# Page loop of a hybrid decoder step: head values, sample products, probability splits and value lower halves are issued in another order

## The reference

```python
def mla_keys(ckv, w_uk, kn_nope):
    return rms_norm(jnp.einsum('...c,chd->...hd', ckv, w_uk), kn_nope)
...
def mla_prompt_attention(q_nope, q_pe, k_nope, k_pe, v):      # 16 heads, 256 tokens, causal
        s = mla_scores(qn, qp, k_nope, k_pe)
        s = jnp.where(k_pos[None, :] <= q_pos[:, None], s, -jnp.inf)
        p = jax.nn.softmax(s, axis=-1)
        return jnp.einsum('bhqk,bkhv->bqhv', p.astype(v.dtype), v)
...
    def page_step(carry, p_idx):                              # 8 requests x 16 cached pages
        phys = page_table[:, p_idx]
        ckv = pool_ckv[phys]
        s = mla_scores(q_nope, q_pe, mla_keys(ckv, w_uk, kn_nope), pool_kpe[phys])
        return merge(carry, s, ckv), None
...
    s = mla_scores(q_nope, q_pe, k_nope_new, k_pe_new)        # the sample's own new position
```

## Time and profile before

| | us |
|---|---|
| time before, median of 3 runs (2768.45 to 2770.84) | 2768.56 |
| the profiled execution, its own time | 2765.64 |
| its span in the trace | 2764.0 |
| PE busy | 2633.9 (95% of the span) |
| DVE busy | 1910.3 (69%) |
| ACT busy | 1341.6 (49%) |

### The profile page before, as it was taken

The page is one execution under the profiler, slowest core; times in us unless marked ns, Lnnn a source line. Parts: engine busy times, 40 slices in busy tenths (PEclk is TensorE's granted clock), DMA queues, the critical chain, the costliest instruction groups (busy, mean ns, idle before and its releaser), DMA issues.

```text
span 2764.0 us, 60668 instructions
## 1 busy us (share of the span) xinstructions
PE 2633.9 (95%) x22232; PEld 2480.3 (90%) x22232; DVE 1910.3 (69%) x3729; ACT 1341.6 (49%) x2759; POOL 227.0 (8%) x327
## 2 busy tenths in 40 slices
PE   7987799999999999999899999979999999999997
PEld 5777689999999999996789999968999999999997
DVE  4656659979996555553667777754997999755554
ACT  2333214457775444443345555541455777544443
POOL 0034100000000000000013333320000000000000
PEclk9999999999999999999899999989999999999999
DMA  5311034544444555554012222213454444455553
GB/s 172 122 54 34 15 122 157 179 166 155 156 158 168 182 182 179 179 213 165 19 36 85 81 81 85 82 47 122 153 178 166 158 156 159 170 179 180 181 182 130
DMA packets 109764, 372.42 MB, mean 135 GB/s; under 512 B 16665, under 2 KB 21018, under 8 KB 109026
## 3 DMA queue, kind: packets, MB, share of 16 engines
q1 hardware_dynamic: 94706, 324.34, 34.0%
q0 software_dynamic: 14832, 45.10, 5.3%
HBM read 365.36 MB, written 4.01 MB: 134 GB/s over the span
## 4 chain that ended last, share of the span: by engine, by line
PE 86%; DVE 8%; ACT 3%; issue 2%; DMA 0%; DVEq 0%; ACTq 0%; POOL 0%; SPq 0%; POOLq 0%
PE ps L795 84%; ACT arena L2273 2%; DVE arena L1496 2%; DVE arena L2092 1%; DVE ring_lo L1496 1%; PE ps L1094 1%; PE ps L1089 1%; DVE arena L1625 0%; DVE arena L1500 0%; DVE arena L2123 0%; DVE v_lo L1496 0%; PE ps L854 0%; ACT L2273 0%; DVE arena L1511 0%; DMA cst<-in_consts 0%
## 5 line engine op out<-in xcount | busy, mean ns | idle before, releaser
L1496 DVE TENSOR_TENSOR ring_lo<-ring,w_hi 128x1024 fp32r<-128x1024 f32 x512 | 624.8, 1223 | 397.7 <-ACT w_hi L2273 394.2
L2273 ACT ACTIVATE arena<-ps 128x256 f32<-128x256 f32 (+18 forms) x981 | 399.1, 426 | 777.6 <-PE ps L795 702.5
L2273 ACT ACTIVATE w_hi<-ring 128x1024 fp32r<-128x1024 f32 x512 | 542.3, 1059 | 385.8 <-PE ps L795 384.7
L795 PE MATMUL ps<-x_hi,w_hi 128*128 128x264 f32 x2048 | 592.8, 289 | 2.8 <-DVE ring_lo L1496 2.8
L795 PE MATMUL ps<-x_hi,ring_lo 128*128 128x264 f32 x2048 | 582.2, 284 | 0.0
L795 PE MATMUL ps<-x_lo,w_hi 128*128 128x264 f32 x2048 | 582.1, 284 | 0.0
L795 PE MATMUL ps<-h_lo,w_hi 128*128 128x264 f32 x2048 | 582.0, 284 | 0.0
L795 PE MATMUL ps<-h_hi,ring_lo 128*128 128x264 f32 x2048 | 581.7, 284 | 0.0
L795 PE MATMUL ps<-h_hi,w_hi 128*128 128x264 f32 x2048 | 579.8, 283 | 1.0 <-issue 1.0
L1496 DVE TENSOR_TENSOR arena<-arena 128x512 f16<-128x512 f16 (+19 forms) x738 | 402.1, 564 | 17.6 <-DVE arena L1496 3.3
L795 PEld LDWEIGHTS ps<-x_hi,w_hi 128*128 128x128 f32 x2048 | 386.6, 189 | 4.3 <-issue 4.2
(11 more groups left out here) (170 smaller groups left out, 2760.9 us busy)
## 6 DMA issues: line engine op xcount, KB each, us to landing
ring<-in_wstream SPq DMA_DIRECT2D x608, 512.0 KB, 3.3
arena<-in_cache_t POOLq DMA_DIRECT2D x128, 128.0 KB, 2.3
arena<-in_cache_n POOLq DMA_DIRECT2D x128, 128.0 KB, 2.3
arena<-in_mla_w POOLq DMA_DIRECT2D x1, 3072.0 KB, 10.2
arena<-in_state POOLq DMA_DIRECT2D x4, 512.0 KB, 4.3
out_wkv_s<-arena POOLq DMA_DIRECT2D x4, 512.0 KB, 4.7
arena<-in_cache_t SPq DMA_DIRECT2D x128, 16.0 KB, 1.7
arena<-in_consts SPq DMA_DIRECT2D x1, 1472.0 KB
```

Source lines behind the costliest of these rows:

```text
L795: return nc.tensor.matmul(out, lhsT, rhs, start=start, stop=stop, **kw)
L1496: return v.tensor_tensor(out, a, b, op)
L2273: return nc.scalar.activation(out, in_, func, **kw)
```

## The change

Four edits, all in the page loop:

1. `products` on PE: six matmuls in the place of 32, two of 64 columns (all heads of one parity in one matmul) and four of 32 columns, into the same bank with the same result. It now stands behind the first third of page 17.
2. `head_values`: on PE head n - 2 behind the first third of page n, in the place of head n - 1 at the end of page n. On DVE head n - 2 ahead of `head_scores(n)`, in the place of head n - 1 behind it.
3. `lower_value` on DVE: right behind `page_sums`, in the place of the end of the loop pass.
4. `prob_sums` is cut in two: `split_probs` at the end of the pass of p = 8, the sum of the probabilities stays at p = 9.

```diff
--- before.py
+++ after.py
@@ -1318,10 +1318,13 @@
 
                 w.next(heads_ready)
                 take(6)
-                for h in range(HEADS):
-                    o = ps[:, 6, h * NS:(h + 1) * NS]
-                    mm(o, C(f"half{h % 2}"), prodn[:, h // 2, :], True, False)
-                    last = mm(o, C(f"quar{h % 4}"), prodr[:, h // 4, :], False, True)
+                acc = dict(skip_group_check=True)
+                by_half = ps[:, 6, 0:P].rearrange("p (c f b) -> p f c b", f=2, b=NS)
+                by_quarter = ps[:, 6, 0:P].rearrange("p (g m b) -> p m g b", m=4, b=NS)
+                for f in range(2):
+                    mm(by_half[:, f], C(f"half{f}"), prodn, f == 0, False, **acc)
+                for m in range(4):
+                    last = mm(by_quarter[:, m], C(f"quar{m}"), prodr, False, m == 3, **acc)
                 last.then_inc(for_dve, 1)
 
             def head_scores(h):
@@ -1413,8 +1416,6 @@
             for b in (1, 2, 4, 5):
                 pe.wait_ge(bank_free[b], taken[b])
             for n in range(PAGES):
-                if n == HEADS + 1:
-                    products()
                 req, p = n // NPAGE, n % NPAGE
                 q = req - 1
                 if p == 0 and req >= 2:
@@ -1423,6 +1424,10 @@
                 pe.wait_ge(pg_ready, n + 1)
                 take(3 * (n % 2), 2)
                 third_keys(n, 0)
+                if 2 <= n < HEADS + 2:
+                    head_values(n - 2)
+                if n == HEADS + 1:
+                    products()
                 if q >= 0:
                     if p == 4:
                         turn_max(q)
@@ -1444,8 +1449,6 @@
                     head_turns(n - 1)
                 if n < HEADS:
                     head_scores(n)
-                if 1 <= n <= HEADS:
-                    head_values(n - 1)
             for j in range(2):
                 for half in range(2):
                     b = 2 * j + half
@@ -2148,13 +2151,16 @@
                 own(tt(sm(3, q), sm(3, q), sm(4, q), ALU.subtract))
                 tell(pr_in)
 
-            def prob_sums(q):
+            def split_probs(q):
 
                 w.next(pr_exp)
                 pair = p_pair[q % 2]
                 own(v.tensor_copy(pair[:, :, 0:HEADS], PR[q]))
                 own(tt(pair[:, :, HEADS:2 * HEADS], PR[q], pair[:, :, 0:HEADS].bitcast(F32), ALU.subtract))
                 tell(pp_ready)
+
+            def prob_sums(q):
+
                 own(v.tensor_reduce(sm(5, q), PR[q].rearrange("p g h -> p h g"), AX.X, ALU.add))
                 tell(sum_ready)
 
@@ -2201,21 +2207,22 @@
             for n in range(PAGES):
                 req, p = n // NPAGE, n % NPAGE
                 q = req - 1
-                if n == HEADS + 1:
-                    products()
                 if n + 2 < PAGES:
                     page_lower(n + 2)
+                if 2 <= n < HEADS + 2:
+                    head_values(n - 2)
+                    if n == HEADS + 1:
+                        tell(o_ready)
+                        products()
                 if n < HEADS:
                     head_scores(n)
-                if 1 <= n <= HEADS:
-                    head_values(n - 1)
-                    if n == HEADS:
-                        tell(o_ready)
                 if n + 1 < HEADS:
                     masked_query(n + 1)
                 if q >= 0 and p == 9:
                     prob_sums(q)
                 page_sums(n)
+                for m in ahead_of(n):
+                    lower_value(m)
                 if q >= 0:
                     if p == 0:
                         key_roots(q)
@@ -2234,14 +2241,15 @@
                     tell(uk_ready)
                 if q >= 1 and p == 5:
                     value_rows(q - 1)
-                for m in ahead_of(n):
-                    lower_value(m)
+                if q >= 0 and p == 8:
+                    split_probs(q)
             key_roots(NS - 1)
             value_rows(NS - 2)
             request_scores(NS - 1)
             spread_max(NS - 1)
             request_out(NS - 2)
             shift_scores(NS - 1)
+            split_probs(NS - 1)
             prob_sums(NS - 1)
             inverse_sums(NS - 1)
             value_rows(NS - 1)
```

## The result

| | before | after |
|---|---|---|
| time, median of 6 runs each | 2768.51 (2762.82 to 2771.26) | 2782.31 (2778.95 to 2791.0) |
| ratio, 95% interval | | 1.0044 (1.0026 to 1.0062) |
| the profiled execution, its own time | 2765.64 | 2782.1 |
| page loop, us | 509.15 | 522.53 |
| page loop up to PE's last values | 500.11 | 513.30 |

The changed kernel is slower by 13.8 us in the medians; 2782 was forecast. It is the better yardstick for a part of the change, since two executions of one kernel differ by several us elsewhere: in the profiled execution of after, the loop begins 2.9 us later than in that of before, behind code that is the same. Of the 16.5 us between the two profiled executions, 13.4 lie in the page loop.

A forecast was written before the change was run, and what follows sets the result against it. PE was busy nearly all the time, with PE and DVE both nearly full in the head stage; +16.8 - 4.4 + 2.1 - 0.6 - 0.3 = +13.6 us took 2768.56 to 2782, 8 in 10 within 2772 to 2790.

The forecast's parts named there:

- The ring: Head stage: DVE's whole page, bank 7's release and PE's turns and scores follow serially, 6.88 us a page; +16.8 us.
- Page 20: Behind the head stage: PE idles 8.7 us because page 20's keys load late, behind the value rows; -4.4 us.
- The clock: Pages 20 and 21 run at half speed behind PE's idle 8.7 us; +2.1 us; head stage costs nothing.
- Products: On PE: six calls make 12 records of 1.4 to 2.3 us, taking 10 to 11 us from PE.
- Requests: Changes of request: earlier value lower halves gain only 0.1 us each, because bank copies limit PE; -0.6 us over six.
- The split: Earlier probability split at p = 10: gains nothing except for the last request but one; -0.3 us.
- Sum: Whole kernel: all terms together add +13.6 us, taking the median from 2768.56 to 2782.
- A free ring: Rival for the head stage: the new ring does not bind, so the kernel gets faster, 2762; 4%.
- loads that don't hold page 20: Rival at page 20: -13.1 us in the place of -4.4 and no cold start, 2771; 6%.
- request gaps in full: Rival at changes of request: all waits for v_lo and split go, some 15 us, 2768; 4%.
- a lower clock in the head stage: Rival: the clock falls in the head stage, ring 8.2 us, +19 us more, 2801; 5%.

The follow-up runs named there:

- e1: Changed kernel with the head values back in their old places on PE and DVE; median 2763.83 us, ratio 0.9970.
- e4: Changed kernel with PE's order kept, but DVE's head values right behind masked_query, ahead of page_sums; median 2760.24 us, ratio 0.9953.
- e2: Changed kernel with 32 product matmuls instead of six, in the new place; median 2784.17 us, ratio 1.0053.
- e3: Changed kernel with POOL issuing the keys of pages 20 to 23 ahead of its wait for o_ready; median 2769.64 us, ratio 0.9999.
- e10: Kernel before the change, with only the keys of pages 20 to 23 issued ahead of the wait for o_ready; median 2772.79 us, ratio 1.0004.
- e7: Changed kernel with the value lower halves back at the end of the loop pass; 2788.71 us, one run.
- e8: Changed kernel with the split of the probabilities back at p = 9; 2788.0 us, one run.
- e5: Changed kernel with the edits of e1 and e3 together; median 2758.59 us, ratio 0.9960.

## Why the prediction was right

- **The ring.** Forecast 6.88 us a page, measured 6.85 (6.97 in every fourth). The three legs: 4.77 from the score step to the end of the values (4.8 said; 4.89 in every fourth page), 0.21 to PE's start (0.24), 1.87 to the next score step (1.84). Stage: +16.28 us where +16.8 stood. e1 and e4 show that it is DVE's order that makes it: with DVE's values ahead of page_sums the ring still exists, but its legs are then 2.81, 0.21 and 1.87, 4.9 us, shorter than PE's own page of 5.15.
- **Page 20.** Last head's values done 9.4 us after the last score step (9.6 said), page 20 on PE at 24.07 (24.5), hole 8.22 (8.7): -4.87 where -4.4 stood. e2, e3 and e10 confirm the cover that the old products gave.
- **The clock.** Half through 5.21 us behind the hole; pages 20 to 23 lose 2.4 by it (14.66 us against 12.23 in e3). +2.1 said, from 3 to 5.3 us at half speed; it was the longer end, the one that the earlier trace rows shows, while the 3 had no row behind it. The head stage kept 1.00, as the stretch at 77% in the earlier trace rows let expect.
- **Products.** 18 records take 1.92 us, six of them the values, which take 0.6 in a head page: 1.3 us for the 12, just under the 1.4 to 2.3 given, since all ran at the full clock.
- **Requests.** The copy sets the pace: -0.6 forecast over six changes. The periods show 0.06 each between before and after and 0.09 between e7 and after, so -0.3 to -0.5. The 0.84 ahead of p = 3 was named; the 0.58 ahead of p = 4 was in the arithmetic but not told as a wait. The split was costed at -0.3, all of it for the last request but one, and page 122 shows 0.33.
- **Sum.** +13.6 forecast. Up to the last values the loop grew by 13.19: 16.28 in the stage, -4.87 up to page 20, +2.37 in pages 20 to 37, -0.28 in the next 80 pages and -0.31 behind them. Each term is within 0.6 us of its forecast, two too high and two too low, so the misses partly cancel. That the median moved by 13.8 is luck to that digit: its interval reaches from 7 to 17 us.
- **Rivals.** A free ring (2762) falls by the 6.85, loads that don't hold page 20 (2771) by ACT's wait of 11.24 for them and by e3, request gaps in full by the periods of e7 and e8, a lower clock in the head stage by the window.

What I had wrong was PE's own page: 5.4 us of work stood in the text; e4, without any wait on PE, needs 5.15 for most heads and 5.21 in the mean. It did not enter the sum, because DVE's ring set the pace, but it misjudged e4's head stage by 4 us (3 under before expected, 7.0 measured). e4's median, 2760.24, met the expected 2760.5 all the same, which is luck: up to the last values its loop is 13.1 us under before's, its median 10.2. And it hid what the move on PE was worth: with DVE's part left where PE's values wait for nothing, 7.0 us of stage (79.94 to 72.94), not "at most 3".

## What to carry to other kernels

When work moves later on one engine, follow what its end frees: a bank given back last in DVE's page turned two nearly full engines into one ring of both, and the cure was to move the release, not the work. When slow work is removed, look up which load it covered and what that load is queued behind; here ten saved microseconds became an eight-microsecond wait. With the head values ending sooner a part of them counts (e1, 4.3 us for the three other edits), and nearly all of them with the earlier load as well (e5, 10.8). The length of a wait is not its worth: 1.29 us of waiting for v_lo were worth 0.09, since a bank stood right behind, while 0.33 us less of waiting for the split were worth nothing six times and 0.33 the seventh, where three pages of values followed.

## What was not expected of the hardware

A short wait on PE cost more than the idle time that the profile shows. In before each head page has one wait of 0.22 us; in e4 it is gone and the page is 0.50 us shorter (79.94 less 72.94, over 14). The rows say where the rest sits: in e4 the eight score matmuls start at 1395.48 and the next keys already at 1396.61, 1.13 later, though the group is 1.48 long, so 0.35 of it overlap. Where the next matmul waits, it starts behind the modelled end and the overlap is lost too. The wait was thus 0.57 from start to start; other small shifts give back 0.07. No run has the head values right behind the scores without a wait, so the overlap is read from the keys that follow there.

Back-to-back small matmuls went with a lower granted clock although PE shows as busy throughout: in e2 it fell to 0.50 at 1459.3, 3 us into 70 records back to back, and rose only after 4.4 us of large matmuls; with 18 such records, in after, it stayed at 1.00.
